# Second half of each attention unit's probabilities weighed on GpSimd

## What is computed

```
s_w = jnp.einsum('bqgrd,bkgd->bgrqk', qb, kwb)
s_w = s_w - slopes[...] * d_w                       # ALiBi: a slope per head, d_w the distance
p_w = _masked_softmax(s_w, m_w)
o_w = jnp.einsum('bgrqk,bkgd->bqgrd', p_w, vwb)
return (gb[:, :, 0, ...] * o_c + gb[:, :, 1, ...] * o_s + gb[:, :, 2, ...] * o_w)
```

## Time and profile before

| | |
|---|---|
| median of three runs | 1552.05 us |
| profiled execution | 1554.86 us, span 1553.0 us |
| PE busy | 1373.6 us, 88% of the span |
| DVE busy | 791.0 us, 51% |
| ACT busy | 438.1 us, 28% |
| GpSimd (POOL) busy | 891.8 us, 57% |
| chain of waits, by engine | PE 68%, DVE 21%, ACT 4%, issue 4%, POOL 2% |
| mean granted TensorE clock | 0.948 |

### The profile page before, as it was taken

One profiled execution on the slowest core, in us unless ns is written; L12 is line 12 of the kernel. 1 busy time (PEld: TensorE's weight loads), 2 busy tenths in 40 slices (PEclk: granted clock), 3 DMA queues, 4 the chain that ended last, 5 costly groups with the idle time before them and its releaser, 6 DMA issues.

```text
span 1553.0 us, 23072 instructions
## 1 busy us (share of the span) xinstructions
PE 1373.6 (88%) x8212; PEld 1061.8 (68%) x8212; DVE 791.0 (51%) x1386; ACT 438.1 (28%) x815; POOL 891.8 (57%) x704
## 2 busy tenths in 40 slices
PE   4979878797996899999959999788888979999986
PEld 2758668575885688877728878745555847778874
DVE  3754798416999701186040008668785136742312
ACT  3025620305330103300141111266765041331102
POOL 3859401084997888899527879100000837558972
PEclk8989979899998999999979999889999999999999
DMA  3213100033322443344616333000001519633321
GB/s 147 70 53 96 48 1 3 7 89 85 96 88 88 147 145 96 98 124 130 225 34 190 95 99 105 21 1 1 1 1 42 203 55 225 202 109 95 95 81 61
DMA packets 86048, 137.95 MB, mean 89 GB/s; under 512 B 16464, under 2 KB 34384, under 8 KB 84816
## 3 DMA queue, kind: packets, MB, share of 16 engines
q1 hardware_dynamic: 48384, 88.10, 19.1%
q10 hardware_dynamic: 37584, 48.71, 9.8%
HBM read 119.02 MB, written 20.91 MB: 90 GB/s over the span
## 4 chain that ended last, share of the span: by engine, by line
PE 68%; DVE 21%; ACT 4%; issue 4%; POOL 2%; DMA 1%; DVEq 0%; ACTq 0%; POOLq 0%
PE ps L353 16%; PE ps L355 16%; PE ps L354 16%; PE ps L346 3%; PE ps L662 3%; PE ps L674 2%; PE ps L651 2%; POOL wh L1174 2%; DVE xs L1241 2%; DVE uL L1231 1%; DVE ffL L1578 1%; PE ps L732 1%; PE ps L494 1%; DVE bigB L1671 1%; DVE bigB L1469 1%
## 5 line engine op out<-in xcount | busy, mean ns | idle before, releaser
L1174 POOL TENSOR_TENSOR wh<-raw,small 128x512 fp32r<-128x512 f32 x336 | 402.8, 1199 | 348.7 <-PE ps L355 337.7
L1176 POOL TENSOR_TENSOR wl<-raw,wh 128x512 fp32r<-128x512 f32 x336 | 474.7, 1413 | 26.3
L353 PE MATMUL ps<-uH,wh 128*128 128x512 f32 x800 | 322.8, 403 | 34.7 <-DVE uL L1231 34.6
L354 PE MATMUL ps<-uL,wh 128*128 128x512 f32 x800 | 317.2, 396 | 0.0
L355 PE MATMUL ps<-uH,wl 128*128 128x512 f32 x800 | 316.9, 396 | 0.0
L353 PEld LDWEIGHTS ps<-uH,wh 128*128 128x128 f32 x800 | 153.4, 192 | 81.2 <-issue 28.1
L355 PEld LDWEIGHTS ps<-uH,wl 128*128 128x128 f32 x800 | 153.7, 192 | 32.9
L354 PEld LDWEIGHTS ps<-uL,wh 128*128 128x128 f32 x800 | 154.1, 193 | 31.0 <-issue 0.5
L353 PE MATMUL ps<-ffH,wh 128*128 128x512 f32 x256 | 102.2, 399 | 4.9 <-POOL wl L1176 4.7
L1209 POOL TENSOR_SCALAR bigB<-const_table 128x512 f32<-128x512 f32 x16 | 11.3, 718 | 161.1 <-DVE small L1671 147.8
L354 PE MATMUL ps<-ffL,wh 128*128 128x512 f32 x256 | 100.5, 393 | 0.0
(11 more groups left out here) (343 smaller groups left out, 2299.3 us busy)
## 6 DMA issues: line engine op xcount, KB each, us to landing
raw<-wstream SPq DMA_DIRECT2D x336, 256.0 KB, 2.6
b_powers_scratch<-bigB ACTq DMA_DIRECT2D x4, 1024.0 KB, 5.2
c_powers_scratch<-bigB ACTq DMA_DIRECT2D x8, 512.0 KB, 4.5
lags_scratch<-lag_rows_scratch ACTq DMA_DIRECT2D x8, 512.0 KB, 7.4
bigB<-b_powers_scratch ACTq DMA_DIRECT2D x4, 1024.0 KB, 8.0
bigB<-lags_scratch ACTq DMA_DIRECT2D x4, 1024.0 KB, 5.9
bigB<-c_powers_scratch ACTq DMA_DIRECT2D x4, 1024.0 KB, 8.8
hT<-x ACTq DMA_DIRECT2D x1, 2048.0 KB, 9.1
```

The lines of the kernel that those rows point to most:

```text
L353: pe.matmul(out, lh, rh, start=first, stop=False)
L354: pe.matmul(out, lh, rl, start=False, stop=False)
L1174: pool.tensor_tensor(wh[:, j, :], raw[:, j, :], zero_ap.to_broadcast([128, 512]), ALU.add).then_inc(half_lead, 1)
L1176: pool.tensor_tensor(wl[:, j, :], raw[:, j, :], wh[:, j, :].bitcast(f32), ALU.subtract).then_inc(half_split, 1)
```

## The change

`weigh` on DVE keeps the reciprocal, the product with the gate and the first half's product. Its product with the gate now raises a semaphore `at_w`. GpSimd waits for `at_w` and multiplies the second half in place, and raises `at_p2`; PE's turn waits for `at_p` and for `at_p2`. The slope products, which stood in GpSimd's program as one row of 16, are now made in between: those of t = 0 and 1 at first, those of t+1 ahead of the product of unit 0 of t.

```
@@ PE, turn(u)
                 pe.wait_ge(at_p, u + 1)
+                pe.wait_ge(at_p2, u + 1)
@@ GpSimd
-            for n in range(NH):
-                t, half = n // 2, n % 2
+            def slopes(t):
                 if t >= 2:
                     pool.wait_ge(at_s, 8 * (t - 1))
-                pool.tensor_scalar(dsl[t % 2][:, half, :], const("dist"), const("slope")[...], 0.0,
-                                   ALU.mult, ALU.add).then_inc(ds_ready, 1)
+                for half in range(2):
+                    pool.tensor_scalar(dsl[t % 2][:, half, :], const("dist"), const("slope")[...], 0.0,
+                                       ALU.mult, ALU.add).then_inc(ds_ready, 1)
+
+            slopes(0)
+            slopes(1)
+            for u, (t, qt, b) in enumerate(UNITS):
+                if t and t + 1 < KT and qt == 0 and b == 0:
+                    slopes(t + 1)
+                W = (qt + 1) * 128
+                pool.wait_ge(at_w, u + 1)
+                pool.tensor_scalar(prob[:, u % 3, 1, 0:W], prob[:, u % 3, 1, 0:W], asum[:, u % 3, 1:2], 0.0,
+                                   ALU.mult, ALU.add).then_inc(at_p2, 1)
@@ DVE, weigh(u)
-                own(dve.tensor_tensor(asum[:, u % 3, :], asum[:, u % 3, :], gate[:, qt, 1 + b, t::KT], ALU.mult))
-                for half in range(2):
-                    i = dve.tensor_scalar(prob[:, u % 3, half, 0:W], prob[:, u % 3, half, 0:W], asum[:, u % 3, half:half + 1], None, ALU.mult)
-                i.then_inc(at_p, 1)
+                dve.tensor_tensor(asum[:, u % 3, :], asum[:, u % 3, :], gate[:, qt, 1 + b, t::KT], ALU.mult).then_inc(at_w, 1)
+                dve.wait_ge(at_w, u + 1)
+                dve.tensor_scalar(prob[:, u % 3, 0, 0:W], prob[:, u % 3, 0, 0:W], asum[:, u % 3, 0:1], None, ALU.mult).then_inc(at_p, 1)
```

More of the change, by code:

```diff
@@ L263, in build @@
         ds_ready = sem("slopes_ready")
-        at_qk, at_s, at_m, at_e, at_p, at_t, at_ev, at_v, at_o = (sem(f"att_{n}") for n in
-            ("scores", "scores_read", "max", "exp", "probs", "transposed", "probsT", "value", "out"))
+        at_qk, at_s, at_m, at_e, at_w, at_p, at_p2, at_t, at_ev, at_v, at_o = (sem(f"att_{n}") for n in
+            ("scores", "scores_read", "max", "exp", "weights", "probs", "probs_second", "transposed", "probsT", "value", "out"))
         s_bc = sem("ssm_bc_loaded")
@@ L1203, in _ @@
             pool.wait_ge(cmp_act, 2)
-            for n in range(NH):
-                t, half = n // 2, n % 2
+            def slopes(t):
                 if t >= 2:
                     pool.wait_ge(at_s, 8 * (t - 1))
-                pool.tensor_scalar(dsl[t % 2][:, half, :], const("dist"), const("slope")[:, half * 8 + t:half * 8 + t + 1], 0.0,
-                                   ALU.mult, ALU.add).then_inc(ds_ready, 1)
+                for half in range(2):
+                    pool.tensor_scalar(dsl[t % 2][:, half, :], const("dist"), const("slope")[:, half * 8 + t:half * 8 + t + 1], 0.0,
+                                       ALU.mult, ALU.add).then_inc(ds_ready, 1)
[8 more added lines that the diff above has]
+                                   ALU.mult, ALU.add).then_inc(at_p2, 1)
             split_weights(2 * SLOT0["nout"] + RING, 2 * NSLOT)
```

## The result

The changed kernel took 1559.95 us (median of 8 runs, 1558.40 to 1561.54), the kernel before 1553.0 us in its 8 runs. The ratio is 1.0038 [1.0029, 1.0047]: slower by about 5.9 us (the two medians lie 6.95 apart; the ratio is estimated from all the runs), where 3.8 us less were forecast, and outside the range given, 1544 to 1557. The profiled executions took 1561.54 us (span 1559.8) and 1554.86 us (span 1553.0), a difference in span of 6.8.

What follows compares the result with a forecast made beforehand. It took the attention's chain of waits, shared by PE and DVE, as the bound. Six heads at -0.66 (-4.0) and two at +0.08 (+0.2) gave -3.8: 1551.1 us profiled, 1548.2 at the median, range 1544 to 1557.

Steps and rivals of the forecast that it cites:

- step 7: After weigh 6: GpSimd's waiting product goes before L1231, which ends some 0.55 us later, hidden in PE's gapless stretch.
- first rival: After weigh 6: DVE keeps the port for L1231, turn 6 comes 0.53 us later per head; 1552.5 us in sum, chance 0.17.
- step 6: Slope products move behind the head's last weigh: the 0.74 us stall goes, 0.14 is added, net -0.60 a head.
- step 3: Hand-over from DVE's product through GpSimd's to PE's turn: later by 0.14, 0.08, 0.01 us for 512, 384, 256 keys.
- A: Stretch of a warm head from shift 3 to turn 4, 6.82 us; forecast -0.06.
- step 4: Shift 3 to turn 4: shift 5 gains 0.14 us, turns 2 and 4 come 0.01 and 0.08 later, net -0.06.
- B: Stretch from turn 4 to shift 7, set by PE, 3.03 us; forecast unchanged.
- D: Stretch from turn 6 to the next head's shift 3, PE without a gap, 7.90 us; forecast unchanged.
- step 5: Turn 4 to shift 7: no change; PE's third wait costs nothing, otherwise +0.25 us a head.
- C: Stretch from shift 7 to turn 6, set by DVE, 3.49 us; forecast -0.60.
- slower rival: GpSimd's product costs more than forecast, on the path at turns 2, 4 and 6: 1556.5 to 1560.0 us, chance 0.20.
- the dip to 0.86: One head at mean granted clock 0.86 took 3.0 us more; forecast to come or stay away in a run.

Runs made afterwards that it cites:

- after: The changed kernel (half the weighing and the moved slopes on GpSimd) against the kernel before: 1559.95 us, ratio 1.0038.
- GpSimd's product first: Changed kernel with L1242 moved behind shift 1 of the next head, and PE's turn waiting for at_p2 first: 1547.95 us, ratio 0.9964 to the kernel before.
- Rest moved: Changed kernel with the rest of the finished head (L1242) moved from behind weigh 6 to behind shift 1 of the next head: 1548.96 us, ratio 0.9961 to before.
- rest waits: Changed kernel where DVE waits for GpSimd's product of unit 6 before the rest of the finished head (L1242): 1549.63 us, ratio 0.9978 to before.
- wait order: Changed kernel where PE's turn waits for at_ev first, then at_p, and at_p2 last: 1564.65 us, ratio 1.0053 to before.
- last head on DVE: Changed kernel with both halves of the eighth head (units 56 to 63) weighed on DVE as before: 1556.59 us, ratio 1.0015 to before.
- pause: Kernel before with slopes behind the last weigh, plus four extra DVE products of 512 ahead of the last head's weigh 6: 1548.61 us, ratio 0.9972.
- slopes only: Kernel before with GpSimd making the slopes behind the head's last weigh, all weighing on DVE: 1547.09 us, ratio 0.9953.

## Why the prediction was wrong

**The step that failed** is step 7: "GpSimd has been waiting and should go first". It doesn't. L1242 follows DVE's product directly on the same engine, starts 0.40 after it, and GpSimd's product, which had waited since 0.06 after the start of the same product, comes behind both and ends 1.56 after DVE's product starts; over 1.2 was the prediction's own sign of being wrong. That is the first rival's mechanism, to which I gave 0.17, and its size, 0.53 a head, was right: the experiments give 21.28 - 20.77 = 0.51. Moving the rest away, or making it wait, gives it back. (The rival charged it to all eight heads, +4.2; L1231 stands behind weigh 6 in seven of them, so its 0.53 is +3.7.) I had weighed the right argument for it (L1231 is issued before the product ends) against a weaker one: in the split stage GpSimd's turns between DVE's operations don't show that it is served first when DVE's next operation is already there. That DVE then always goes first isn't shown either: the runs have one such pair, L1696 and L1242.

**The slopes** (step 6) were right. Alone they give 0.74 a head; in after they lie behind the last weigh and nothing waits for them. They come 1.36 after turn 6 (1.61 with GpSimd's product first, where turn 6 isn't late) and not 2.4: my count was too late, on the safe side.

**The hand-over** (step 3) was right in kind and too small by 0.07 to 0.12. From the start of DVE's product to the turn:

| keys | before | forecast | measured | of it the semaphore | of it GpSimd's own time |
|---|---|---|---|---|---|
| 512 | 0.94 | 1.08 | 1.15 | +0.05 | +0.02 |
| 384 | 0.80 | 0.88 | 0.97 | +0.05 | +0.04 |
| 256 | 0.67 | 0.68 | 0.80 | +0.05 | +0.07 |

The turn starts 0.10 after GpSimd's end in after, not 0.05, since the wait is second in a row of three. GpSimd's end lies 0.56, 0.45 and 0.35 after DVE's for 512, 384 and 256 keys (0.54, 0.41, 0.28 forecast); with the 0.15 ahead of the port its own times are 0.71, 0.60 and 0.50, against the 0.69, 0.56 and 0.43 of the line through the earlier trace rows. The line's fixed part was drawn from a copy and is too small. These own times are worked out from the rule; no run has GpSimd's product while DVE is idle, so how its 0.98 divides into waiting and work is not measured. The rule itself (GpSimd ends at DVE's end plus its own time less 0.15) held roughly also behind L1242: 0.48 after its end against 0.54.

**A** (step 4): shift 5 came 0.17 sooner after turn 2 (2.36 against 2.53), where 0.14 was forecast, but turn 2 came 0.13 and turn 4 0.17 later, so +0.12 instead of -0.06. With only units 0, 1, 3 and 5 on GpSimd this gain stays and its price goes: -0.15. **B and D** (step 5) each came 0.03 shorter, since a turn that waited for the second semaphore is recorded 0.03 shorter.

So a warm head: C -0.74 + 0.21 + 0.51 = -0.02, A +0.12, B and D -0.06; 0.04 in sum, as measured. The first rival had 21.1 for it; with the three undersized terms it is 21.28.

Between the forecast of 3.8 less and the 6.8 more of the profiled execution lie 10.6. By the traces this is, as an estimate: the port in seven heads, 7 x 0.51 = 3.6; the hand-over and what it does to A, B and D, some 1.4; the low clock behind the last turn 6, 2.7; the single delay, 0.4; and 2.4 outside the attention that is not shown to be the change's. Rest moved and rest waits, which take away the first term alone, have no low clock behind the last turn 6 (8.09 from there to L353 in both), so the failed step stands behind 6.3 of the 10.6. That the median, 1559.95, fits the slower rival's upper figure of 1560.0 is chance: GpSimd's own time is 0.02 to 0.07 over the forecast, not 0.41.

**The clock.** "If the dip to 0.86 comes or stays away in a run, that is 3.0 either way" was the other fault: I treated it as chance, and it goes with the wait of PE. In the ten profiled executions, PE's wait before turn 6, from the second head on, and whether the granted clock fell to 0.50 within 1.4 after that turn's start:

| wait before turn 6 | where | clock fell |
|---|---|---|
| 1.94 to 3.13 | after twice, wait order twice, last head on DVE once, pause once | 6 of 6 |
| 1.58 to 1.64 | before, after, last head on DVE, wait order | 1 of 20 |
| up to 1.49 | all the rest | 0 |

The one of the middle row is before's third head, behind whose turn 6 the slow stretch of the earlier trace rows begins:

```profile
1081.07 1.10 PE L662 MATMUL ps<-const_table,bigB 128*128 128x128 f32 x8 [1.60 <-DVE bigB L1685]
```
```profile
1082.00:1083.00 1.00, 1.00 (x11) 0.91 (x11) 0.90 (x7) 0.80 (x1) 0.00 (x0) 0.57 0.00 0
```

The wait is no sharp limit. Ahead of L353 PE waits 2.18 in every one of the ten, and in eight the clock falls during that wait or within 1.3 after it, in slopes only and pause not at all. The kernels that took the slopes out of C and kept L1242 off GpSimd's product of unit 6 wait at most 1.49 there and have no such head; against before's trace that is 3.1 us beside their shorter period. In the attention's turns after has two low stretches: one at 1166.44, where the single delay of 0.36 lengthens the wait to 1.94, and one in the eighth head, where the wait is 1.28 + 0.73 = 2.01. The last is shown by experiment (gone with the last head on DVE, with the rest moved and with the rest waiting, there again with a pause). For the ones inside the attention it is a pattern over ten executions, in which no kernel changed the wait of a middle head alone. The single delay by itself doesn't bring it: rest moved and product first have it too, their waits are 1.42 and 1.38 there, and the clock stays at 1.00.

**What stays open.** The delay of 0.36 before the seventh head's shift 7 is in after, rest moved, last head on DVE, wait order and product first, and in no other; I don't know its cause. The time behind the attention is 354.9 to 358.1 in the ten executions (356.0 in before, 358.1 in after), in no order that follows the edits; so after's +2.1 there is not shown to be the change's. The mean granted clock of this part is 0.97 in before and 0.96 in after, but also 0.96 in rest moved (357.9). How often the stretches at the low clock come in executions without a trace isn't known.

## What to carry to other kernels

Work moved from VectorE to GpSimd on a path where the next engine waits for both is not halved: here GpSimd's part ended 0.35 to 0.56 after VectorE's of the same size, and an operation with two SBUF inputs that VectorE had ready went ahead of it in each of seven heads. Put such an operation elsewhere, or let it wait. Look first at what else the move rearranges: here nearly the whole gain was one wait on GpSimd's queue (0.74 a head), and the moved work was worth 0.15 a head, and only in the units that nobody waits for. And where a profile shows a stretch at the low clock, read what TensorE waited for right before it, since shortening that wait can be worth more than the wait: 0.73 less of it gave 3.45 here.

## What the runs showed of the hardware that was not expected

- VectorE keeps the port over two operations in a row although GpSimd has been waiting: GpSimd's product of 512 is recorded as 1.50 with L1242 behind DVE's product and as 0.98 without. L1703, as long but with one input in PSUM, leaves the product of 256 at its 0.64.
- The place of a wait in PE's row of waits counts: with the open one first, second or third of three, the turn starts 0.06, 0.10 or 0.15 after GpSimd's end.
- The granted clock fell to 0.50 behind each of six waits of TensorE of 1.94 or more before turn 6, and the low stretch was shorter after 3.13 (1.46 lost) than after 2.01 (2.73 lost). It fell behind one of twenty waits of 1.58 to 1.64, and at eight of ten waits of 2.18 ahead of L353.
